# Transposes of the selected keys as ordinary products with the identity matrix, in the sample stage of a hybrid decoder step

## The reference, cut to what matters

```python
ks_blk = to_blocks(concat([gather(c_sk), ks]), SEL_BLOCK)          # 64 blocks of 64 past keys, and the new key
_, idx = lax.top_k(score, 16)
ks_g = ks_blk[bidx, idx]
ls = einsum('bqhd,bqkd->bqhk', q, ks_g) * scale + rel_bias(...)
p_s = masked_softmax(ls, dist_s >= 0)
o_s = einsum('bqhk,bqkd->bqhd', p_s, vs_g)
```

## Time and profile before

| what | value |
|---|---|
| time, median of 3 runs | 2354.99 us (2348.19 to 2358.0) |
| the profiled execution's own time | 2357.29 us |
| its span, first to last instruction | 2355.5 us |
| mean granted TensorE clock | 0.89 of full speed |
| PE busy | 2044.3 us (87%) |
| PEld busy | 1459.1 us (62%) |
| DVE busy | 851.3 us (36%) |
| ACT busy | 531.5 us (23%) |
| POOL busy | 442.0 us (19%) |

### The profile page before, as it was taken

The page is one execution under the profiler, slowest core; times in us unless marked ns, Lnnn a source line. Parts: engine busy times, 40 slices in busy tenths (PEclk is TensorE's granted clock), DMA queues, the critical chain, the costliest instruction groups (busy, mean ns, idle before and its releaser), DMA issues. The chain is left out here.

```text
span 2355.5 us, 26080 instructions
## 1 busy us (share of the span) xinstructions
PE 2044.3 (87%) x9964; PEld 1459.1 (62%) x9964; DVE 851.3 (36%) x1413; ACT 531.5 (23%) x1132; POOL 442.0 (19%) x548
## 2 busy tenths in 40 slices
PE   5999999984899788888699999999999949999991
PEld 2345555543766666687598878778744337777771
DVE  1233232222243565446476555552211141111113
ACT  1112222221266344422212122121110001111110
POOL 0000000000146422010112322321000023333323
PEclk9889999995699789955899999999999959999996
DMA  8010000001021211074455655553331039999116
GB/s 302 1 47 24 24 24 24 24 21 41 23 90 55 72 37 36 2 279 150 154 151 175 216 188 178 178 187 105 112 103 56 36 137 421 372 355 362 67 49 236
DMA packets 140937, 301.34 MB, mean 128 GB/s; under 512 B 28420, under 2 KB 92589, under 8 KB 127213
## 3 DMA queue, kind: packets, MB, share of 16 engines
q0 software_dynamic: 43840, 197.23, 22.8%
q1 hardware_dynamic: 97006, 102.85, 13.6%
HBM read 294.88 MB, written 36.59 MB: 141 GB/s over the span
## 5 line engine op out<-in xcount | busy, mean ns | idle before, releaser
L801 PE MATMUL PS<-arena,OT 128*128 128x492 f32 (+1 forms) x720 | 338.6, 623 | 11.2 <-ACT small L502 7.5
L1995 PE MATMUL PS<-rows_high,gate_high 128*128 128x344 f32 x768 | 261.9, 341 | 16.3 <-DVE rows_low L2117 16.3
L1997 PE MATMUL PS<-rows_high,gate_low 128*128 128x344 f32 x768 | 248.3, 323 | 0.0
L1996 PE MATMUL PS<-rows_low,gate_high 128*128 128x344 f32 x768 | 248.3, 323 | 0.0
L801 PEld LDWEIGHTS PS<-arena,OT 128*128 128x128 f32 (+1 forms) x720 | 135.3, 194 | 180.3 <-issue 162.6
L1995 PEld LDWEIGHTS PS<-rows_high,gate_high 128*128 128x128 f32 x768 | 147.5, 192 | 46.0 <-issue 39.3
L1996 PEld LDWEIGHTS PS<-rows_low,gate_high 128*128 128x128 f32 x768 | 147.0, 191 | 2.0
L1997 PEld LDWEIGHTS PS<-rows_high,gate_low 128*128 128x128 f32 x768 | 147.1, 191 | 0.0
L2251 PE MATMUL PS<-TT,small 128*128 128x512 f32 (+1 forms) x288 | 136.9, 638 | 1.5 <-PEq L193 1.5
L2001 PE MATMUL PS<-OT,small 128*128 128x344 f32 x384 | 126.5, 452 | 0.0
L2554 PE MATMUL PS<-TT,OT 128*128 128x256 f32 x512 | 118.9, 387 | 6.6 <-DMA arena_last<-in_w_eu,small 5.2
(11 more groups left out here) (499 smaller groups left out, 3279.9 us busy)
## 6 DMA issues: line engine op xcount, KB each, us to landing
gate<-in_w_in SPq DMA_DIRECT2D x32, 512.0 KB, 5.5
slot_rows<-small SPq DMA_DIRECT2D x32, 512.0 KB, 3.2
arena<-in_w_in SPq DMA_DIRECT2D x5, 1968.0 KB, 19.0
OT<-in_x_prompt SPq DMA_DIRECT2D x8, 512.0 KB, 4.6
hT_scratch<-OT SPq DMA_DIRECT2D x8, 512.0 KB, 3.8
small<-in_w_branch SPq DMA_DIRECT2D x32, 128.0 KB, 6.9
arena_last<-in_x_prompt SPq DMA_DIRECT2D x8, 512.0 KB
normed_rows<-arena_last SPq DMA_DIRECT2D x8, 512.0 KB, 2.6
```

The lines of the kernel that those rows point to most:

```text
L801: last = MM(bank(PBANK[c])[0:R, 0:CH], hTs[:, j, 0:R], W1[:, j, c * CH:(c + 1) * CH], start=(j == 0), stop=(j == KD - 1))
L1995: MM(G, H[:, k, :], hTh[:, k, cols], start=(k == 0), stop=False)
L1996: MM(G, H[:, k, :], hTl[:, k, cols], start=False, stop=False)
L1997: MM(G, L[:, k, :], hTh[:, k, cols], start=False, stop=(k == KD - 1))
```

## The change

In `turn` the transposes become matrix products with the same operands: the keys stationary, the identity matrix moving, written to the same places in PSUM, with `start=True, stop=True`. The waits, the order and the semaphores stay.

```diff
@@ -1551,9 +1551,10 @@
                 flat = Ks[b % NKR].rearrange("p a b -> p (a b)")
                 if g < NKT - 1:
                     for n in range(4):
-                        last = TR(bank(1 + i % 2)[:, n * 128:n * 128 + 128], flat[:, (4 * g + n) * 128:(4 * g + n) * 128 + 128], ident)
+                        last = MM(bank(1 + i % 2)[:, n * 128:n * 128 + 128], flat[:, (4 * g + n) * 128:(4 * g + n) * 128 + 128], ident,
+                                  start=True, stop=True)
                 else:
-                    last = TR(bank(1 + i % 2)[0:64, 0:128], flat[:, 32 * 64:33 * 64], ident)
+                    last = MM(bank(1 + i % 2)[0:64, 0:128], flat[:, 32 * 64:33 * 64], ident, start=True, stop=True)
                 last.then_inc(S3["kt_tp"], 1)
```

## The result

The changed kernel takes 2361.7 us, the median of 15 executions (2356.3 to 2374.7); the kernel before, run beside it, 2354.2 (2348.2 to 2358.5). The ratio, estimated over all executions of both and so not quite the quotient of the medians, is 1.0038, interval 1.0025 to 1.0051: 6 to 12 us slower, a small but certain loss. The forecast was 2349, 6 us faster, with a range of 2333 to 2368 that holds the result; its sign was wrong.

The account below looks back on a forecast made before the run. PE bounds the sample stretch, at clock 0.50. Extra records add 29 us at the low clock, minus 58 s for the high-clock share; s = 0.6 gives -6 us, 2357.3 to 2351.3 profiled, median 2349, range 2333 to 2368.

Parts of the forecast that it names:

- What bounds the stage: Sample stretch: PE, busy 95.53 of 96.4 us, so each microsecond it gains or loses enters the span one for one.
- Records: Sample stretch: a transpose is one record, a 32-bit product two; 17 more per sample, 136 in all.
- Prices: Samples: a record costs 0.21 to 0.22 us at the low clock, 0.11 at the high, whatever it is.
- the end with all at the high clock: Sample stretch with every record at the high clock (s = 1): 67 us together, -29 us.
- hold for one or two: Samples: the clock rises at the head of some, stays high for one or two samples, falls at a thin end.
- the second rival: Samples: clock rises in sample 0 or 1 and stays; -17 to -29 us, median 2326 to 2338; chance 0.18.
- The share s: Sample stretch: share of PE's records at the high clock, chosen as 0.6, giving -6 us.
- two pairs of samples and about one more: Samples taken as high, 5 of 8, for s = 0.6; 3 and 4, 5 and 6 likeliest to stay high.
- the prediction's own formula: Sample stretch: time difference is 29 - 58 s us, s being the share of PE's records at the high level.
- The mixed clock: Sample stretch: s from 0.35 to 0.8, +9 to -17 us, median 2338 to 2364; chance 0.64.
- The wait at L1598: PE's wait for DVE in the sample stretch, 0.8 us before, expected to grow; 1 to 2 us put on it.

Follow-up runs that it names:

- the run with wide scores: Changed kernel (turns as products) with score products 128 moving columns wide instead of 8, against the kernel before: 2331.6 us against 2355.2, ratio 0.9888.
- the two half changes: Changed kernel with turns 0 and 1 transposes again: 2374.2 us, 1.0076; with only turns 0 and 1 as products: 2346.9 us, 0.9960, both against the kernel before.
- the half change: Only turns 0 and 1 of each sample as products, turns 2 to 4 transposes, against the kernel before: 2346.9 us, ratio 0.9960.

## Why the prediction went wrong

- **What bounds the stage: right.** The samples' stretch grew by 10.1 us, what lies behind it by nothing (45.7 us both times), and no wait was added.
- **Records: right.** Two for a product, one for a transpose; 612 counted, 612 forecast.
- **Prices: nearly right, both a little low.** The low sample was put at 14.4 us and took 15.0: 10.8 + 17 x 0.213 leaves out 0.6. It belongs to the product turns that stand behind a narrow score. With only the pair as products a record costs 0.20, with only the turns behind scores 0.29. Why it costs more there was not tested. A sample all high was put at 7.5 us and took 8.4 in the run with wide scores; of the difference some 0.4 are the wide scores (four times 0.09), and where the rest, some 0.5, comes from was not tested. So the end with all at the high clock was too low as well: the stage took 75.0 us at 0.98, not 67. "Every record of this stage costs 0.21 to 0.22" leaves out the products of 64 x 64 between the samples: 32 of them take 1024.63 - 1021.03 = 3.60 us at the low clock, 0.11 each, which the sum did not need.
- **The clock's behaviour: half right.** With 8-column scores it rises with the sixteen wide records at the head and not without, as the two half changes show (0.50 throughout without them, rises with them alone), and it falls around thin ends. That it would "hold for one or two" samples was wrong: no rise lasted longer than 6.9 us, less than one sample. Transposes do not keep it down, against the second rival's page (0.92 with every turn a transpose); that they count as much as products was not shown by itself.
- **The share s: wrong, and this is the step that failed.** I put s at 0.6: "two pairs of samples and about one more". It was 230 of 612 records (those that started at the high clock), 0.38. By the prediction's own formula, 29 - 58 x 0.38 = +7; with the low sample's 0.6 us in four samples, +9.6, for a measured +10.1. So of the 16 us between -6 and +10, 13 are the share (58 x 0.22) and 2.4 the price. Two things in "two pairs" were wrong. Samples 3 and 4 both had a rise, but not one: between them the clock fell for 3.4 us (1059.9 to 1063.3), though nothing stands between the two; samples 5 and 6 had none. And a rise comes late in its sample: a sample with one has 2.6 to 4.4 us at the low clock first and takes 9.25 to 10.1 us, which is a saving of 1.2 and not of 3.3. Four rises held 230 records, so a share of 0.6, 367 records, would have taken a rise in six of the eight samples; the prediction counted whole samples as high.
- **The chances.** The mixed clock was given shares from 0.35 to 0.8, and yet 0.03 of it below 0.3; the measured 0.38 lies near its lower end.
- **Softer points.** The wait at L1598 did not grow (0.51 us for 0.80): the sample ahead of it was low and took 15.0 us, which left DVE more time. It did grow, to 2.13 us, in the kernel with wide scores and transposes.

**What stays open.** The same sixteen records raised the clock in samples 0, 3, 4 and 7 and not in 1, 2, 5 and 6, and in the half change in others again (0, 1, 2, and 6 with 7). No run tells what picks them. It fits with the spread of the executions of the changed kernel (2356 to 2375 us, against 2348 to 2359 before), but this was not followed execution by execution.

## What to carry to other kernels

Where PE is busy all the time and its clock stands at 0.50, look at the moving columns before the form of the instructions: here products with 8 columns, alternating with turns, held a whole stage at the low clock, and streaming the same columns sixteen times over, in the same instructions, took 34 us off. In the table's products over 33 rows the same trick took nothing off, and where only the end of each sample was widened, with transposes, it gained nothing. Leave 32-bit transposes as transposes; as products they are twice the records, and what clock they won here was had without them. A forecast that counts on the clock should price a unit of work that starts low and rises within itself, not one that is wholly high or low.

## What I had not expected of the hardware

- Surplus columns up to 128 cost little with 32-bit operands: eight records of a score take 0.90 us with 128 columns and 0.81 with 8, both at the high clock. At the low clock the eight of score 3 take 1.85 us wide (1053.51 to 1055.36 in the kernel with transposes and a wide end) and 1.65 narrow (1058.49 to 1060.14 before).
- Columns are not all: products over 33 rows, with 128 columns, left the clock at 0.50 for 29 us.
- More records took less time where the clock was up: 612 in 75.0 us (0.98), 476 in 96.4 us (0.50).
